# Chunked scan of a hybrid layer: the part carried by the state computed token by channel and turned on TensorE

## The reference, cut to what matters

```
a_cum = cumsum(dt * a)                                   # per token and head
y_diag = einsum(cb * decay * dt, x)                      # inside the chunk
states = einsum(b_mat, decay_to_end * dt, x)             # what the chunk adds to the state
y_off  = einsum('bclgn,bcgrpn,bclgr->bclgrp', c_mat, prev, exp(a_cum))   # carried by the state
y = y_diag + y_off + d_skip * x
ssm = gated_group_rmsnorm(y, z)                          # y * silu(z), norm over each group
```

## Time and profile before

| what | value |
| --- | --- |
| time, median of 3 runs | 1550.25 us (1548.08 to 1550.91) |
| the profiled execution's own time | 1549.37 us |
| its span, first to last instruction | 1547.6 us |
| TensorE matmul busy | 1517.4 us, 98% |
| VectorE, GpSimd, ScalarE busy | 1051.6, 781.3, 716.0 us (68, 50, 46%) |
| mean granted TensorE clock | 0.996 of full speed |
| chain that ended last, by engine | PE 81%, DVE 10%, issue 2%, ACT 2%, DMA 2%, POOL 2% |
| DMA | 280.64 MB, mean 181 GB/s |

### The profile page before, as it was taken

One profiled execution on the slowest core, in us unless ns is written; L12 is line 12 of the kernel. 1 busy time (PEld: TensorE's weight loads), 2 busy tenths in 40 slices (PEclk: granted clock), 3 DMA queues, 4 the chain that ended last, 5 costly groups with the idle time before them and its releaser, 6 DMA issues.

```text
span 1547.6 us, 22730 instructions
## 1 busy us (share of the span) xinstructions
PE 1517.4 (98%) x7919; PEld 1307.4 (84%) x7919; DVE 1051.6 (68%) x1729; ACT 716.0 (46%) x1445; POOL 781.3 (50%) x686
## 2 busy tenths in 40 slices
PE   9999999999999999899999999999999999999997
PEld 8999998878888889788887888788888888888885
DVE  5856516256878778777778789765565677747676
ACT  5232211245656555566664554444444445444542
POOL 7534444134767766953321425776666135405653
PEclk9999999999999999999999999999999999999999
DMA  6444622226556545798878642454444696535666
GB/s 219 113 138 127 181 55 62 68 63 191 167 166 173 163 131 171 236 338 310 313 283 298 238 165 94 149 177 150 150 150 150 218 380 229 192 110 192 195 197 150
DMA packets 225796, 280.64 MB, mean 181 GB/s; under 512 B 21400, under 2 KB 148224, under 8 KB 225696
## 3 DMA queue, kind: packets, MB, share of 16 engines
q1 hardware_dynamic: 224688, 275.69, 54.8%
q0 software_dynamic: 1008, 3.67, 1.3%
HBM read 180.63 MB, written 98.66 MB: 180 GB/s over the span
## 4 chain that ended last, share of the span: by engine, by line
PE 81%; DVE 10%; issue 2%; ACT 2%; DMA 2%; POOL 2%; SPq 0%; DVEq 0%; ACTq 0%; POOLq 0%
PE ps L2981 19%; PE ps L2972 16%; PE ps L825 7%; PE ps L884 6%; PE ps L2842 5%; PE ps L1801 3%; PE ps L2918 3%; PE ps L840 2%; PE ps L856 2%; PE ps L1717 2%; PE ps L1739 2%; PE ps L458 1%; DVE pTlo L2020 1%; PE ps L1769 1%; PE ps L1786 1%
## 5 line engine op out<-in xcount | busy, mean ns | idle before, releaser
L2981 PE MATMUL ps<-dw_hi,df_hi 128*128 128x512 f32 x448 | 174.5, 389 | 1.6 <-DVE dw_lo L3568 1.6
L2981 PE MATMUL ps<-dw_lo,df_hi 128*128 128x512 f32 x448 | 174.3, 389 | 0.0
L2981 PE MATMUL ps<-dw_hi,df_lo 128*128 128x512 f32 x448 | 174.3, 389 | 0.0
L178 POOL TENSOR_TENSOR ring<-stage,zero 128x512 fp32r<-128x512 f32 (+2 forms) x75 | 83.7, 1116 | 150.8 <-DMA stage<-w_in 47.9
L3563 DVE TENSOR_TENSOR df_lo<-df_raw,df_hi 128x512 fp32r<-128x512 f32 x112 | 114.2, 1020 | 49.6 <-ACT df_hi L3259 48.5
L3568 DVE TENSOR_TENSOR dw_lo<-dw_raw,dw_hi 128x512 fp32r<-128x512 f32 x96 | 80.6, 840 | 43.8 <-ACT dw_hi L3268 26.4
L3259 ACT ACTIVATE df_hi<-df_raw 128x512 fp32r<-128x512 f32 x112 | 70.3, 627 | 71.8 <-DMA df_raw<-d_f 71.6
L180 POOL TENSOR_TENSOR ring<-stage,ring 128x512 fp32r<-128x512 f32 (+2 forms) x75 | 100.5, 1340 | 5.9
L2981 PEld LDWEIGHTS ps<-dw_hi,df_hi 128*128 128x128 f32 x448 | 84.1, 188 | 19.5 <-DVE df_lo L3563 2.0
L2981 PEld LDWEIGHTS ps<-dw_lo,df_hi 128*128 128x128 f32 x448 | 84.1, 188 | 17.5
L2981 PEld LDWEIGHTS ps<-dw_hi,df_lo 128*128 128x128 f32 x448 | 84.1, 188 | 17.4
(11 more groups left out here) (543 smaller groups left out, 4536.8 us busy)
## 6 DMA issues: line engine op xcount, KB each, us to landing
df_raw<-d_f SPq DMA_DIRECT2D x112, 256.0 KB, 2.7
d_f<-fa SPq DMA_DIRECT2D x105, 256.0 KB, 2.1
dw_raw<-w_mlp_down SPq DMA_DIRECT2D x96, 256.0 KB, 3.0
landA<-w_mlp_up SPq DMA_DIRECT2D x52, 256.0 KB, 3.2
stage<-w_in SPq DMA_DIRECT2D x40, 256.0 KB, 2.7
stage<-w_out SPq DMA_DIRECT2D x28, 256.0 KB, 5.3
xt<-x SPq DMA_DIRECT2D x8, 512.0 KB, 6.9
d_xT<-xdT SPq DMA_DIRECT2D x8, 512.0 KB, 3.3
```

The costliest lines, as they stand in the source:

```text
L178: pool.tensor_tensor(hi, src, k.zero[:, 0:1].broadcast_to([P, width]), ALU.add).then_inc(k.sem(fam + "_hi"), 1)
L2981: mm = pe.matmul(ps[:, base + t, :], F_AT[q % SLOTS][a][:, P * t:P * t + P], W_AT[q % SLOTS][b][:, :], start=(fresh and (a, b) == (0, 0)), ...
```

## The change

`carried` is computed with tokens on partitions and channels along the row: C is the stationary operand and the state the moving one, 2 groups x 3 passes = 6 matmuls of 512 columns. The decay is then one number per partition and head; ScalarE makes `from_start` = exp(a_cum) for all eight chunks in one activation of 128 x 128 ahead of the scan, and VectorE multiplies PSUM by it, broadcast over a head's 64 channels, into `t1`. `turned_back` turns `t1` with 8 transposes of 128 x 128 into banks 0 and 1, and VectorE adds the 1024 columns from PSUM to `y`, behind `w_low` 2. GpSimd's adds of `t1`, the products `along` with their selector `sel`, and the exponential into `eb` are gone. On TensorE `turned_back(t)` stands behind the second piece of attention; `update(t)` moves behind `diag(t, 1)` and `decays(t, 3)` and waits for VectorE's add (semaphore `s_ya`) instead of its multiply (`s_t1`); on VectorE `state_add` moves behind `mul` 3. In the last chunk `mm_unit(0)` waits for the eighth `s_ya`.

```diff
-def along_products(pe, k, t):
-    by_parity = k.run[t // 4][:, :, :].rearrange("p (a e) l -> p e a l", e=2)
-    for b in range(2):
-        for e in range(2):
-            mm = pe.matmul(k.ps[:, b, :], k.sel[:, t % 4, e, :], by_parity[:, e, 4 * b:4 * b + 4, :], start=(e == 0), stop=(e == 1))
-    mm.then_inc(k.sem("s_eb"), 1)
...
-        act.wait_ge(sem("s_eb"), 1)
-        act.activation(k.eb[:, :], ps[:, 0:2, :].rearrange("p a b -> p (a b)"), ACT.Exp).then_inc(sem("s_E"), 1)
+        act.activation(k.from_start[:, :, :], k.acum[:, 0:NT, :], ACT.Exp).then_inc(sem("s_E"), 1)
...
             pool.wait_ge(sem("s_y1"), 4 * t + 2 * g + 2)
-            pool.wait_ge(sem("s_t1"), t + 1)
-            pool.tensor_tensor(part, part, half(t1, g), ALU.add).then_inc(sem("s_ya"), 1)
-            pool.wait_ge(sem("s_ya"), 2 * t + g + 1)
+            pool.wait_ge(sem("s_ya"), t + 1)
...
         def carried(t):
-            pe.wait_ge(sem("s_E"), t + 1)
             pe.wait_ge(sem("s_stlo"), t + 1)
+            for g in range(GROUPS):
+                for a, b in PASSES:
+                    mm = pe.matmul(ps[:, g, :], cT[a][:, g, :], half(sth[b], g), start=(a == 0 and b == 0), stop=(a == 1))
+            mm.then_inc(sem("s_off"), 1)
+
+        def turned_back(t):
+
+            pe.wait_ge(sem("s_t1"), t + 1)
             for j in range(KD):
-                for a, b in PASSES:
-                    mm = pe.matmul(ps[:, j // 4, P * (j % 4):P * (j % 4) + P], sth[a][:, P * j:P * j + P], cT[b][:, j // 4, :],
-                                   start=(a == 0 and b == 0), stop=(a == 1))
-            mm.then_inc(sem("s_off"), 1)
+                mm = pe.transpose(ps[:, j // 4, P * (j % 4):P * (j % 4) + P], t1[:, P * j:P * j + P], k.ident[:, :])
+            mm.then_inc(sem("s_back"), 1)
...
         def update(t):
-            pe.wait_ge(sem("s_t1"), t + 1)
+            pe.wait_ge(sem("s_ya"), t + 1)
...
             if t:
                 similar(t)
                 decays(t, 0)
-                along(t)
...
             attention(t, 5, 8 if t else 7)
+            turned_back(t)
+            diag(t, 1)
+            decays(t, 3)
             if t:
                 update(t)
-            diag(t, 1)
-            decays(t, 3)
-            if t == 0:
+            else:
                 attention(t, 7, 8)
             diag(t, 2)
...
             if i == 0:
-                pe.wait_ge(sem("s_t1"), NT)
+                pe.wait_ge(sem("s_ya"), NT)
...
                 expo(t, 0)
-                act.wait_ge(sem("s_eb"), t + 1)
-                act.wait_ge(sem("s_t1"), t)
-                act.activation(eb[:, :], ps[:, 0:2, :].rearrange("p a b -> p (a b)"), ACT.Exp).then_inc(sem("s_E"), 1)
                 w_hi(t, 0)
...
             dve.wait_ge(sem("s_off"), t + 1)
-            dve.wait_ge(sem("s_E"), t + 1)
             if t:
-                dve.wait_ge(sem("s_ya"), 2 * t)
-            dve.tensor_tensor(t1[:, :], ps[:, 0:2, :].rearrange("p a b -> p (a b)"), eb[:, :], ALU.mult).then_inc(sem("s_t1"), 1)
+                dve.wait_ge(sem("s_back"), t)
+            else:
+                dve.wait_ge(sem("s_E"), 1)
+            dve.tensor_tensor(heads(t1[:, :]), heads(ps[:, 0:2, :].rearrange("p a b -> p (a b)")), by_head(k.from_start[:, t, :]), ALU.mult).then_inc(sem("s_t1"), 1)
             w_low(t, 1)
...
             w_low(t, 2)
-            if 0 < t < LAST:
-                state_add(t)
-            elif t == LAST:
+            dve.wait_ge(sem("s_back"), t + 1)
+            dve.wait_ge(sem("s_y1"), 4 * t + 1)
+            dve.tensor_tensor(y[:, t % 2, :], ps[:, 0:2, :].rearrange("p a b -> p (a b)"), y[:, t % 2, :], ALU.add).then_inc(sem("s_ya"), 1)
+            if t == LAST:
                 w_cuts(RING + STAGES + 2, RING + KD)
             skipped(t, 1)
             mul(t, 3)
+            if 0 < t < LAST:
+                state_add(t)
             w_low(t, 3)
```

More of the change, by code:

```diff
@@ L539 @@
 v_cut s_ya s_y1 s_xw_in s_xh_in1 s_xD_in1 s_xD_in0 s_wm s_wlo s_whi s_t1 s_stp s_ssv s_ssq s_sqr s_sq s_sent s_seg s_run1 s_off s_mixc
-s_mix_sent1 s_mix_sent0 s_mix s_gz s_glo s_gh s_exp s_eb s_dg s_dec s_cb s_at_in1 s_at_in0 s_at_first s_E m_x_in m_weighted m_w_in m_v m_turned m_sqrt
+s_mix_sent1 s_mix_sent0 s_mix s_gz s_glo s_gh s_exp s_back s_dg s_dec s_cb s_at_in1 s_at_in0 s_at_first s_E m_x_in m_weighted m_w_in m_v m_turned m_sqrt
 m_sq m_sent1 m_sent0 m_scaled m_rs m_part m_mm m_mix_in1
@@ L1335, in scan_maps @@
     k.bt, o = pair("s_bt", [P, GROUPS * STATE], o)
-    k.sel, o = m.at("sel", [P, 4, 2, P], F32R, o)
+    k.from_start, _ = m.at("from_start", [P, NT, SH], F32, o)
+    o += 4 * 4 * 2 * P
     k.zs, o = m.at("s_z", [P, SSMW], F32, o)
@@ L1674, in on_gpsimd @@
         pool.memset(k.one[:, :], 1.0).then_inc(sem("s_one"), 1)
[L1675 to L1682, removed]
         pool.wait_ge(sem("p_xwhi"), 1)
@@ L1884, in on_tensor @@
         turn(HEADS - 1, NT - 1, False)
-        pe.wait_ge(sem("s_sel"), 2)
+        pe.wait_ge(sem("s_pick"), 1)
         pe.wait_ge(sem("s_run"), SH // 4)
-        along_products(pe, k, 0)
         weigh(HEADS - 1, HEADS // 2 - 1, 1, 1, LATE_OUT)
@@ L2209, in w_turn @@
         return n // STAGES + (2 if RING + STAGES <= n < FAR else 1)
-    bT, cT, bt, sel, zs, pick, one = k.bT, k.cT, k.bt, k.sel, k.zs, k.pick, k.one
+    bT, cT, bt, zs, pick, one = k.bT, k.cT, k.bt, k.zs, k.pick, k.one
     y, o = m.at("s_y", [P, 2, SSMW], F32, k.o_scan)
@@ L2221, in phase_rest @@
     assert o == o_acc
-    eb, o = m.at("eb", [P, SSMW], F32, o + 320)
+    o += 320 + 4 * SSMW
     mixs, o = m.at("mixs", [P, D], F32, o)
     wl, o = pair("wl", [P, 2, 4, P], o)
-    k.eb, k.wl, k.y, k.xwh = eb, wl, y, xwh
+    k.wl, k.y, k.xwh = wl, y, xwh
     o_early = o
@@ L3372, in skipped @@
                 dve.wait_ge(sem(f"s_xD_in{t % 2}"), 16 * (t // 2 + 1))
+            else:
+                dve.wait_ge(sem("s_ya"), t + 1)
             for e in range(2):
```

3 lines of the change are left out of this document (removed).

## The result

The changed kernel takes 1565.59 us (median of 4 runs, 1564.83 to 1566.77) against 1550.26 for the kernel before (4 runs, 1548.08 to 1550.91): ratio 1.0098, 95% interval 1.0085 to 1.0110. It is slower, as forecast, but by 15.3 us where 7.5 was forecast, and above the range of 1547 to 1562. The profiled execution took 1566.77 us, with a span of 1565.0.

A forecast was written before the change was run, and what follows sets the result against it. TensorE was taken as the bound, busy 21.09 of 21.09 us in a middle chunk. Chunk 0 -0.35, six chunks +5.3 and last chunk +2.5 gave +7.5 on 1550.25: 1557.8 us, range 1547 to 1562.

The forecast's parts named there:

- TensorE's saving, -1.29 per chunk: TensorE per chunk: `along` gone -0.94, `carried` in six wide matmuls -1.23, eight new transposes +0.88; net -1.29 us.
- The wait of 2.2 us at `update` in chunks 1 to 6: TensorE at `update` waits 2.2 us for VectorE's add, against 1.29 saved: +0.9 each, +5.3 us for six chunks.
- `mm_unit(0)` 2.5 later: Last chunk: `mm_unit(0)` waits for the eighth add, and the shift goes through to the end: +2.5 us.
- Chunk 0, -0.35: Chunk 0: `update` finds the add done; the projection copy TensorE waits for comes earlier with `decays(0, 3)`: -0.35 us.
- Its going makes that wait longer and brings 0: Ahead of the scan: removing the first `along` only lengthens TensorE's 0.99 us wait for VectorE; effect 0.
- The clock stays at 1.00: TensorE keeps the 2.4 GHz level behind every wait, citing a clock of 1.00 over 3.6 us of idling; nothing added.
- rival 4: Clock falls to 1.2 GHz in the waits, half rate behind each, +14 us: 1572; chance 0.01.
- rule on transposes: Skill's rule for the eight new transposes: not counted as array activity, so a stall beside them could lower the clock; unpriced.
- the add is in time: At `update`: the add is done in time and the saved columns remain, -8.1 us, 1542.2; chance 0.11.

The follow-up runs named there:

- e6: Changed kernel without VectorE's add; what waited for it waits for the multiply, and the output lacks the carried part: 1542.10 us.
- e5: Kernel before, with only one wait added: `update` in chunks 1 to 6 also waits for VectorE's third low part: 1566.39 us.
- e8: Changed kernel with unused matmuls in TensorE's waits: four ahead of the scan, eight ahead of each `update`, thirteen ahead of `mm_unit(0)`: 1554.50 us.
- e2: Changed kernel with each chunk's eight transposes replaced by four plain matmuls of 512 columns, carried part left out of the output: 1565.50 us.
- e9: e7 with `turned_back` and the add of chunk 0 back behind the steps they follow in the change: 1543.18 us.
- e1: Changed kernel with four unused matmuls ahead of the scan, where the first `along` had stood: 1565.14 us.
- e3: Changed kernel with `update` moved behind `diag(t, 2)` and three more attention blocks, and `state_add` behind `w_low` 3: 1554.72 us.
- e4: Changed kernel with the add ahead of `skipped` 0 and `mul` 2, `turned_back` earlier, `diag(t, 2)` later, ScalarE's mix copy and last chunk's multiply earlier: 1548.63 us.
- e7: e4 with filling matmuls ahead of the scan, chunk 0's `diag(0, 2)` back in place, and GpSimd's `run[1]` moved to chunk 2: 1544.40 us.

## Why the prediction was wrong

The sign was right, and so was the mechanism of the waits; the size was half. The step that failed is the clock: the forecast kept it at 1.00 behind every wait, and lower clocks brought more than half of the loss. Step by step:

- *TensorE's saving, -1.29 per chunk.* Right. Six starts of `carried` 0.234 apart (694.54 to 695.71), eight transposes in 0.79 us (700.37 to 701.16) with 0.1 more to the second start behind them; without the add the chunk is 1.38 shorter. The multiply with the broadcast decay takes 1.22 us, the add 1.21, both as taken.
- *The wait of 2.2 us at `update` in chunks 1 to 6.* Right. The forecast reckoned in starts, and in starts it is 22.00 - 19.71 (e6) = 2.29. The brackets say 1.94 to 2.03, which is idle time alone: the matmul ahead of a wait counts with its full length (0.40 in place of 0.23), and the first one behind it is 0.33 from the next (682.35, 682.68). That is why a chunk grows by 0.91 and not by 2.01 - 1.38. With the clock kept up these six chunks cost +5.0 (5.3 forecast). The earlier trace rows were enough for this.
- *`mm_unit(0)` 2.5 later.* Nearly right: it waits 3.40 us (3.7 forecast), and the last chunk is 2.14 longer when the wait is filled. Measured 3.7: the rest, 1.56, is the clock.
- *Chunk 0, -0.35.* Right: -0.46. The rows below are attention's first matmuls in the scan, in the kernel before, the changed one, e5 and e8. From there to `similar` of chunk 1 (667.38, 669.28, 669.37, 668.90) it is 20.23, 19.77, 20.25 and 19.77 us. TensorE's wait for the copy of the mix grew from 0.38 to 0.88, because TensorE gets there 1.0 us earlier and the copy is done only 0.5 earlier. That e8's whole stretch is as long as before all the same (31.13 against 31.16) is because it had lost 0.43 ahead of the scan.

```profile
647.15 2.31 PE L2842 MATMUL ps<-ring,s_aT 128*128 128x512 f32 x9
649.51 2.31 PE L2823 MATMUL ps<-ring,s_aT 128*128 128x512 f32 x9
649.12 2.31 PE L2844 MATMUL ps<-ring,s_aT 128*128 128x512 f32 x9
649.13 2.31 PE L2825 MATMUL ps<-ring,s_aT 128*128 128x512 f32 x9
```

- *"Its going makes that wait longer and brings 0"*, of the first `along`. Here the first step failed. The wait grew as it said, from 0.99 to 2.08 us, but TensorE then ran for 4.82 us at the 1.2 GHz level. The rows above start 10.93, 13.20, 11.43 and 11.36 us behind `similar` of chunk 0: 2.27 lost by the changed kernel, and 1.84 of them gone with matmuls in `along`'s place (e8). These do not hold the fall off: in e8 the four themselves take 1.91 us, at the low level. But this lies in time that would have been waited, and the matmuls behind them start 0.23 apart from 644.69 on, where the changed kernel gets there at 647.2. `along` itself does not hold it off either: e5 has it, fell there all the same, and lost 0.5. Of the eleven profiles only that of the kernel before has no fall there. So what is shown is that the removal lets a fall be paid in full; that it brings the fall is not shown.
- *The clock stays at 1.00; rival 4 at a chance of 0.01.* This is the step that cost the range. The rival was put aside with one row, 3.56 us of idling at a clock of 1.00 ahead of the scan. But those were several waits, the largest 1.85 us, and the same stretch came out at 0.95 in e5. One stretch in which nothing fell says that a fall does not always follow; it was read as saying that none does. What the forecast had priced came to -0.46 + 5.02 + 2.14 = 6.7 us in the profiles. The other 9.9 of the 16.6 came with the lower clock: 2.27 ahead of the scan, 6.11 in four of the six chunks, 1.56 in the last one. A fall in the scan costs 1.5 to 1.6, less than the 2 that rival 4 had put, and five of its seven waits had one. e8 shows the cause for the waits in the scan by taking away the idling alone, e5 by adding it alone.

The Trainium skill bears on this in two places. Its rule on transposes (TensorE: Matmul & The Clock Gate, Part 4: PE-mode transpose), which the prediction had weighed, does not explain these falls: e2 has plain matmuls in their place and the same falls. The same page, in the section "HAM oscillation — how this bites in real kernels", tells of a loop that waits in every round and starts the next matmuls at the lower clock. That is the pattern here in four of six rounds. But the waits of its example are longer, about 3 to 5 us by the page; that waits of 2 us do it in a part of the rounds is what these runs show, and no run here has a loop with waits as long as the page's.

Of the rivals, "the add is in time" gave 1542.2. In the chunks that price was right: without the add chunks 1 to 6 are 7.4 us shorter than before, where 7.7 was reckoned. That the median of e6 (1542.1) is the same to 0.1 us is in part luck, since its profile has 2.8 us lost up to chunk 1 and 1.0 gained in the last, neither of them in the sum. e9 (1543.2) has the add kept and moved; the change as written does not get there.

What stays open: what decides which of several equal waits has a fall behind it. Waits of 1.86 to 2.03 us at `update` had one in 4 of 6, 5 of 6, 5 of 6 and 2 of 6 cases (changed kernel, e1, e2, e5); those of 1.36 in e3 had none in 4, and those of 3.37 to 3.41 (at `mm_unit(0)` in the changed kernel, e1, e2 and e3, in chunk 0 in e4) had one in 5 of 5. A shift of all waits by 2 us changed which ones had it, and one stretch had it in one kernel's profile and not in the other's with the same instructions. More was not tried.

## What to carry to other kernels

When a change gives the bounding TensorE a wait of about 2 us in every round of a loop, price it twice: the wait, reckoned in starts, less what is saved, and half the rate for some time behind a part of them (1.5 us each here); take the second from a range between no fall and one behind each, never from a single stretch that kept its clock. Work that is taken out of TensorE ahead of a wait that it cannot avoid is not free of effect: here it was priced at nothing, and 1.8 us came back when other matmuls were put in its place. And when an operation moves onto the path, look first at its place in the order of the engine that does it: with the add behind `w_low` 2 the change costs 15 us, with it ahead of `mul` 2 and the repairs of e7 and e9 it gains 6 to 8.

## What the runs showed of the hardware

At the 1.2 GHz level matmuls of 512 columns start 0.43 us apart, at 2.4 GHz 0.234; the level can change in the middle of a row of six (705.16). Behind a wait of 2.03 us the clock did not fall at once: three matmuls still ran at full rate, and the low level lasted from there for some 3.3 us (worked out from the mean clock of 0.93 over the 23.54 us of chunk 2). Useless matmuls laid into the waits made the kernel faster (1565.6 to 1554.5 us). And the same matmuls in the same order ran at a clock of 1.00 in one profile and 0.95 in another (up to chunk 1, the kernel before and e5).
